# One-hot gather and scatter of a mixture of experts in fp32r, two experts per gather, with the gate applied to the expert's result

## The reference

```
logits = xt @ router_w
top_val, top_idx = top_k(logits, 2)
gates = softmax(top_val)
y_e = (silu(x_e @ w1[e]) * (x_e @ w3[e])) @ w2[e]      # x_e: the tokens that chose expert e
out[token] = sum over its two experts of gate * y_e[token]
```

## Time and profile before

| what | us |
|---|---|
| median of three runs | 2055.57 (2054.56 to 2055.81) |
| profiled execution, first to last instruction (span) | 2052.6 |
| busy: TensorE matmul / VectorE / ScalarE / GpSimd | 1953.8 / 1426.9 / 996.0 / 80.1 |
| expert loop, from the first `up` to the last matmul of the last scatter | 1177.6 to 1995.1 |

### The profile page before, as it was taken

How to read it: one execution, slowest core, us unless ns; L and a number is a source line. 1 busy time by engine, 2 the same in 40 slices (tenths; PEclk the granted TensorE clock), 3 DMA queues, 4 the chain that set the end, 5 groups by cost and what they waited for, 6 DMA issues and landing times. The chain is left out here.

```text
span 2052.6 us, 29833 instructions
## 1 busy us (share of the span) xinstructions
PE 1953.8 (95%) x12519; PEld 1773.6 (86%) x12519; DVE 1426.9 (70%) x1720; ACT 996.0 (49%) x1137; POOL 80.1 (4%) x123
## 2 busy tenths in 40 slices
PE   5988999999998999999999899999999999999998
PEld 4867878878887968999999798989898989898976
DVE  6789996463765346665456488878887888787862
ACT  2511111224366212434355566666666666666654
POOL 3000000000000100100220000000000000000000
PEclk9999999999999999999999999999999999999999
DMA  9845221453432432456753298999898989998970
GB/s 333 267 140 166 85 83 42 156 172 125 143 104 91 158 123 83 145 185 192 211 193 130 95 334 330 342 337 345 333 343 335 341 335 347 333 345 333 342 297 21
DMA packets 225857, 452.29 MB, mean 220 GB/s; under 512 B 6944, under 2 KB 91176, under 8 KB 225720
## 3 DMA queue, kind: packets, MB, share of 16 engines
q1 hardware_dynamic: 222400, 445.44, 61.9%
q0 software_dynamic: 1632, 4.75, 0.8%
q10 hardware_dynamic: 1688, 0.15, 0.1%
HBM read 448.21 MB, written 2.10 MB: 219 GB/s over the span
## 5 line engine op out<-in xcount | busy, mean ns | idle before, releaser
L2002 DVE TENSOR_TENSOR ring_r<-ring,his_r 128x2816 fp32r<-128x2816 f32 (+1 forms) x192 | 586.9, 3085 | 58.4 <-ACT his_r L1543 58.3
L1543 ACT ACTIVATE his_r<-ring 128x2816 fp32r<-128x2816 f32 (+1 forms) x192 | 490.7, 2560 | 193.7 <-DMA ring<-in_moe_w_dram 179.8
L1149 PE MATMUL bank<-his_r,hg_r 128*128 128x352 f32 x2048 | 356.4, 326 | 0.8 <-ACT hg_r L1567 0.8
L1149 PEld LDWEIGHTS bank<-his_r,hg_r 128*128 128x128 f32 x2048 | 334.0, 188 | 1.8 <-issue 0.9
L2475 PE MATMUL bank<-hT,ring 128*128 128x256 f32 x912 | 210.0, 386 | 5.9 <-DVE arena L3053 4.0
L2475 PEld LDWEIGHTS bank<-hT,ring 128*128 128x128 f32 x912 | 171.8, 192 | 33.4 <-issue 10.2
L1149 PE MATMUL bank<-ring_r,hg_r 128*128 128x352 f32 x1024 | 185.9, 323 | 0.0
L1149 PEld LDWEIGHTS bank<-ring_r,hg_r 128*128 128x128 f32 x1024 | 169.0, 188 | 0.0
L3074 DVE SCALAR_TENSOR_TENSOR arena<-ring,cw,arena 128x256 f32<-128x256 f32 x240 | 96.4, 475 | 0.1
L1175 PE MATMUL bank<-his_r,at_hi_r 128*128 128x512 f32 x352 | 93.8, 399 | 0.0
L1175 PE MATMUL bank<-his_r,at_lo_r 128*128 128x512 f32 x352 | 92.5, 396 | 0.0
(11 more groups left out here) (541 smaller groups left out, 2946.1 us busy)
## 6 DMA issues: line engine op xcount, KB each, us to landing
ring<-in_moe_w_dram SPq DMA_DIRECT2D x128, 1408.0 KB, 8.2
ring<-in_moe_w_dram SPq DMA_DIRECT2D x48, 1536.0 KB, 8.7
ring<-in_even_w_in_dram SPq DMA_DIRECT2D x28, 1024.0 KB, 6.5
ring<-in_ffn_w_dram SPq DMA_DIRECT2D x22, 1024.0 KB, 5.3
ring<-in_ada_w_dram SPq DMA_DIRECT2D x20, 1024.0 KB, 10.1
ring<-in_odd_w_in_dram SPq DMA_DIRECT2D x9, 2048.0 KB, 7.8
ring<-in_moe_w_dram SPq DMA_DIRECT2D x16, 1024.0 KB, 6.2
ring<-in_a_w_in_dram SPq DMA_DIRECT2D x6, 2048.0 KB, 8.1
```

Of the source, the lines that this page charges most:

```text
L1149: ins = mm(bank[first + m][:, 0:WC], x[:, KT // 2 * late + k, :], w[:, k, WC * m:WC * m + WC], start=(not late and k == 0 and s == "hg_hi" ...
L1543: A(moe_hi(n), moe_w(n), ACT.Copy).then_inc(sem("moe_hi"), 1)
L2002: V.tensor_tensor(moe_lo(n), moe_w(n), moe_hi(n).bitcast(F32), ALU.subtract).then_inc(sem("moe_lo"), 1)
```

## The change

The gather and the scatter become fp32r products. The tokens are split into `htok_hi_r` (ScalarE) and `htok_lo_r` (GpSimd, four subtractions of 128x512); the one-hot matrix is exact in fp32r. One gather now serves two experts: 256 columns, 32 matmuls, once before the loop and then behind chunk 19 of experts 1, 3 and 5. The scatter multiplies the two parts of the result by a turned one-hot matrix `pick_r`. The gate no longer sits in the matrix: the matrix is turned together with gate columns in a product of 160 columns (`turn_pick`), VectorE sums the gate of each slot (`gate_of_slot`), ScalarE scales by it as it writes the high part of the result, and VectorE makes the low part (`result_lo`). The reciprocals of the router's and the final norm are taken after the turn, over 128x2 instead of 128x256. Before the loop, rank and count products are fewer, `lo(0)`, the gates and the overflow test stand later. The two table loads now count on one semaphore, and both of its readers wait for both loads.

```diff
# SBUF, semaphores of the table loads, GpSimd
+        hg_hi_r = sb_r("hg_hi_r", 0, KT, 2 * SLOTS)
+        hg_lo_r = sb_r("hg_lo_r", 27768, KT, 2 * SLOTS)
+        htok_hi_r = sb_r("htok_hi_r", 4864, TT, D)
+        ys_r = [sb_r("ys_hi_r", 12544, D), sb_r("ys_lo_r", 13568, D)]
...
-            ... a["c_w_s_2"] ... .then_inc(sem("ws_loaded"), 16)
+            ... a["c_w_s_2"] ... .then_inc(sem("spatial_loaded"), 16)
...
-                .then_inc(sem("bs_loaded"), 16)
+                .then_inc(sem("spatial_loaded"), 16)
...
+            for n, (tt, half) in enumerate(TOKEN_ORDER):
+                pool.wait_ge(sem("toks_taken"), TK_H + n + 1)
+                r = slice(512 * half, 512 * half + 512)
+                pool.tensor_tensor(htok_lo_r[:, tt, r], HTOK[:, tt, r], htok_hi_r[:, tt, r].bitcast(F32), ALU.subtract).then_inc(sem("htok_lo"), 1)
# TensorE
-                    pe.wait_ge(sem("ws_loaded"), 16)
+                    pe.wait_ge(sem("spatial_loaded"), 32)
...
+            pe.wait_ge(sem("routed"), 1)
+            mm(bank[1][:, 0:TT * NE], TRI, SEL[:, :, :].rearrange("p u e -> p (u e)"), start=True, stop=False, skip_group_check=True)
+            mm(bank[1][:, NE:TT * NE], ones[:, :], SEL[:, 0, :], start=False, stop=True, skip_group_check=True).then_inc(sem("rank_ready"), 1)
...
+            def gather(n, width):
+                per = 512 // width
                 for ct in range(KT):
+                    if n == 1 and width == 2 * SLOTS and ct % 4 == 0:
+                        pe.wait_ge(sem("htok_lo"), ct // 2 + 2)
...
+                    for x in (htok_hi_r, htok_lo_r):
+                        for tt in range(TT):
+                            ins = mm(o, x[:, tt, ct * P:(ct + 1) * P], s, ...)
...
+            def turn_pick(b, m):
+                for tt in range(TT):
+                    ins = mm(b[:, tt * TURNED:(tt + 1) * TURNED], psel_r[:, tt, m, :], turner_r[:, :], start=True, stop=True)
...
             def scatter(first, done):
                 for ct in range(KT):
-                    ins = mm(bank[first + ct // 2][...], YS[:, ct * P:(ct + 1) * P], GTS, start=True, stop=True)
+                    for y in ys_r:
+                        ins = mm(bank[first + ct // 2][...], y[:, ct * P:(ct + 1) * P], pick_r[...], ...)
...
-                    if j == GATHER_AT and e < NE - 1:
-                        pe.wait_ge(sem("at_lo"), 6 * e + 4)
+                    if j == GATHER_AT and e % 2 == 1 and e < NE - 1:
+                        pe.wait_ge(sem("at_lo"), 6 * e + 6)
+                        pe.wait_ge(sem("psel_ready"), 4 * (e // 2) + 8)
# ScalarE
+            for n, (tt, half) in enumerate(TOKEN_ORDER):
+                act.wait_ge(sem("toks_ready"), TK_H + 4)
+                b, r = bank[(2, 3, 6, 7)[2 * tt + half]], slice(512 * half, 512 * half + 512)
+                A(HTOK[:, tt, r], b[:, :], ACT.Identity, scale=RSC[:, tt:tt + 1])
+                A(htok_hi_r[:, tt, r], b[:, :], ACT.Identity, scale=RSC[:, tt:tt + 1]).then_inc(sem("toks_taken"), 1)
+                if n == 1:
+                    act.wait_ge(sem("routed"), 2)
+                    A(GATE[:, :, :], GATE[:, :, :], ACT.Exp).then_inc(sem("side_exps"), 1)
...
-                    A(YS[...], bank[2 * (e % 2) + half][:, :], ACT.Copy).then_inc(sem("ys_taken"), 1)
+                    A(ys_r[0][...], bank[2 * (e % 2) + half][:, :], ACT.Identity, scale=GSLOT).then_inc(sem("ys_hi"), 1)
# VectorE
-            step(V.reciprocal(nr[:, :], nr[:, :]))
             dve.wait_ge(sem("router_ready"), 1)
-            V.tensor_tensor(RLT[0:NE, :], bank[5][0:NE, 0:T], nr[0:NE, :], ALU.mult).then_inc(sem("norm_scaled"), 1)
-            lo(0)
+            V.tensor_copy(RLT[0:NE, :], bank[5][0:NE, 0:T]).then_inc(sem("norm_scaled"), 1)
             dve.wait_ge(sem("router_ready"), 2)
+            V.reciprocal(RSC, bank[0][:, 2 * NE:2 * NE + TT]).then_inc(sem("norm_scaled"), 1)
...
+            def result_lo(first, n):
+                for half in range(2):
+                    r = slice(512 * half, 512 * half + 512)
+                    dve.wait_ge(sem("ys_hi"), 2 * n + half + 1)
+                    V.scalar_tensor_tensor(ys_r[1][:, r], bank[first + half][:, :], GSLOT, ys_r[0][:, r].bitcast(F32), ALU.mult, ALU.subtract)\
+                        .then_inc(sem("ys_taken"), 1)
...
+            select(0, 0, 0)
+            select(1, 1, 0)
+            dve.wait_ge(sem("rank_ready"), 2)
+            V.tensor_copy(CNT[:, 0, :], bank[0][:, 0:NE]).then_inc(sem("rank_taken"), 1)
+            lo(0)
+            gathered(0)
...
+                    if j == 0 and e >= 1:
+                        result_lo(2 * ((e - 1) % 2), e - 1)
...
-            dve.wait_ge(sem("norm_rooted"), 9)
-            V.reciprocal(nr[:, :], nr[:, :]).then_inc(sem("norm_scaled"), 1)
+            dve.wait_ge(sem("router_ready"), 3)
+            V.reciprocal(RSC, bank[5][:, 0:TT]).then_inc(sem("pair_rooted"), 1)
```

More of the change, by code:

```diff
@@ L91, in build @@
         xT = sb("xT", [P, KT, T])
+        with nc.sbuf_tensor("htok_lo_r", [P, TT, D], F32R) as htok_lo_r:
+            pass
         hT = sb("hT", [P, KT, T])
@@ L94, in build @@
         ones = sb("ones", [P, P])
+        with nc.sbuf_tensor("turner_r", [P, P + 2 * TT * NE], F32R) as turner_r, nc.sbuf_tensor("pick_r", [P, TT, P], F32R) as pick_r:
+            pass
         swap_a = sb("swap_a", [P, P])
@@ L109, in build @@
         stb = segm[:, :]
+        with nc.sbuf_tensor("psel_r", [P, TT, 2, SLOTS], F32R) as psel_r:
+            pass
         hspread = sb("hspread", [P, 2, P])
@@ L1112, in pe_rest @@
-            pe.wait_ge(sem("toks_taken"), TK_H + 4)
-            pe.wait_ge(sem("rank_taken"), 1)
-            def gather(psel, v, done):
-                pe.wait_ge(psel, v)
-                for ct in range(KT):
-                    for tt in range(TT):
-                        ins = mm(bank[6 + ct // 4][:, (ct % 4) * P:(ct % 4 + 1) * P], HTOK[:, tt, ct * P:(ct + 1) * P], PSEL[:, tt, :],
-                                 start=(tt == 0), stop=(tt == 1))
-                    if ct % 4 == 3:
-                        ins.then_inc(done, 1)
+            pe.wait_ge(sem("routed"), 1)
@@ L1125, in scatter @@
+            def turn_pick(b, m):
+                for tt in range(TT):
+                    ins = mm(b[:, tt * TURNED:(tt + 1) * TURNED], psel_r[:, tt, m, :], turner_r[:, :], start=True, stop=True)
+                ins.then_inc(sem("gsel_turned"), 1)
             def scatter(first, done):
                 for ct in range(KT):
-                    ins = mm(bank[first + ct // 2][:, (ct % 2) * T:(ct % 2 + 1) * T], YS[:, ct * P:(ct + 1) * P], GTS, start=True, stop=True)
+                    for y in ys_r:
+                        ins = mm(bank[first + ct // 2][:, (ct % 2) * T:(ct % 2 + 1) * T], y[:, ct * P:(ct + 1) * P],
+                                 pick_r[:, :, :].rearrange("p u t -> p (u t)"), start=(y is ys_r[0]), stop=(y is ys_r[1]))
@@ L1182, in scatter_main @@
                 pe.wait_ge(sem("at_lo"), 6 * e + 6)
-                if e < NE - 1:
-                    pe.wait_ge(sem("hg_lo"), 2 * e + 4)
+                if e % 2 == 1 and e < NE - 1:
+                    pe.wait_ge(sem("hg_lo"), 4 * (e // 2) + 8)
                 scatter(4, sem("scat_ready"))
-            gather(sem("psel_ready"), 2, sem("gather_ready"))
+            pe.wait_ge(sem("psel_ready"), 4)
+            gather(1, 2 * SLOTS)
             for e in range(NE):
@@ L2028, in dve_rest @@
-            dve.wait_ge(sem("gate_exps"), 1)
-            ch.settle()
-            step(V.tensor_tensor(GATE[:, :, :], GATE[:, :, :], SEL[:, :, :], ALU.mult))
-            step(V.tensor_reduce(NEG[:, 0:TT], GATE[:, :, :], AX_X, ALU.add))
-            step(V.reciprocal(NEG[:, 0:TT], NEG[:, 0:TT]))
-            V.tensor_tensor(GATE[:, :, :], GATE[:, :, :], NEG[:, 0:TT].unsqueeze(2).to_broadcast([P, TT, NE]), ALU.mult)\
-                .then_inc(sem("sel_ready"), 1)
-            dve.wait_ge(sem("sel_ready"), 1)
+                .then_inc(sem("routed"), 1)
@@ new lines, in gathered, with gate_of_slot @@
+            def gathered(p):
+                for g in range(4):
+                    dve.wait_ge(sem("hg_hi"), 4 * p + g + 1)
+                    V.tensor_tensor(HG_LO[:, 2 * g:2 * g + 2, :], bank[4 + g][:, :].rearrange("p (k s) -> p k s", k=2),
+                                    HG_HI.bitcast(F32)[:, 2 * g:2 * g + 2, :], ALU.subtract).then_inc(sem("hg_lo"), 1)
+            def gate_of_slot(b, n, e):
+                dve.wait_ge(sem("gts_taken"), n)
+                v = b[:, P:P + TT * (TURNED + 2 * NE)].rearrange("p (u c) -> p u c", u=TT)[:, :, bass.ds(2 * e, 2)]
+                V.tensor_reduce(GSLOT, v, mybir.AxisListType.XY, ALU.add).then_inc(sem("gate_ready"), 1)
@@ new lines, in dve_rest @@
+            select(0, 0, 0)
[4 more added lines that the diff above has]
+            gathered(0)
+            dve.wait_ge(sem("side_exps"), 2)
+            ch.settle()
```

(3 more changed lines are left out.)

197 lines of the change are left out of this document (99 added, 98 removed).

## The result

The kernel after takes 2028.97 us (median of 4 runs, 2024.52 to 2030.28) where the kernel before took 2055.07 beside it (4 runs, 2053.05 to 2055.81): a ratio of 0.9877, 95% interval 0.9865 to 0.9889. The forecast was 2032.0 in a range of 2027 to 2040. The profiled execution has a span of 2027.0 us; against the 2052.6 of before that is −25.6, where the sum said −23.6.

The account below looks back on a forecast made before the run. TensorE was taken to bound the loop, with a chain of waits across engines before and behind it. The terms summed to −23.6 us, from a median of 2055.6 to 2032.0 us, range 2027 to 2040.

Parts of the forecast that it names:

- What bounds the loop: In the expert loop TensorE is busy throughout, 102.4 us per expert, so its work moves the end by its own length.
- (b): In the loop, loads at no more than 347 GB/s become the bound, 99.7 us an expert: +12, 2044; chance 0.06.
- (c): In the loop, loads at 339 GB/s already set the pace and the −24.2 is lost: 2058.6 us; chance 0.02.
- the +0.7 for chunk waits: In the loop, faster slots bring weight loads closer together, so short waits for them add 0.7 us.
- Gathers: In the loop, seven f32 gathers of 3.57 us become three fp32r ones of 3.84: −13.5 us.
- scatters: In the loop, seven scatters go from 3.45 to 1.92 us each: −10.7 us.
- The turned pick: Per expert, two f32 transposes become two fp32r products of 160 columns: 0 change, with +2.7 us kept as possible.
- Rival (a): The narrow product is slow: fp32r at 160 columns costs what f32 does, 2034.7 us; chance 0.35.
- The bias wait: Before the loop, TensorE's transposes wait for both table loads: +2.35 us, plus +0.85 for half a clock drop.
- Ahead of the loop: Routing starts earlier, but the first gather waits for GpSimd's fourth quarter behind `lo(0)`: −0.4 us, between −3 and +2.
- The last scatter: Behind the loop, 0.7 us more wait for the second half, scatter down from 3.73 to 1.92: −1.1 us.
- The final norm: At the end, a 1.76 us reciprocal and 0.18 copy go, a 128x2 reciprocal of 0.17 comes: −1.8 us.

Follow-up runs that it names:

- the narrow gather: Kernel after with each pair's gather cut into 64 products of 128 columns instead of 32 of 256: 2046.96 us, ratio 0.9966.
- f32 scatter: Kernel after with the scatter as one plain f32 product of the result's high part, low part left out: 2038.59 us, ratio 0.9931.
- the run with all idle products: Kernel after with `lo(0)` early, first-load wait only, and unused products during the routing wait and around the last scatter: 2022.35 us, ratio 0.9842.
- the rows stored expert by expert: Kernel after with gathered rows in a separate block per expert instead of 256 columns per pair: 2026.13 us, ratio 0.9867.

## Why the prediction was right, point by point

**What bounds the loop**: right. TensorE is busy throughout the loop, and a piece of it moves the loop's end by its own length, in the narrow gather and the f32 scatter too. Rivals (b) and (c), the loads as the bound, are out: at 358 GB/s TensorE still never waits, and the +0.7 for chunk waits was 0. The Trainium skill ("HBM Reference", the table at its head) gives about 358 GB/s per core; the trace reaches that over a whole expert and goes past it, to 394 in a window of 2.3 us (in the run with all idle products), so it wasn't a limit here.

**Gathers**, forecast −13.5: −12.9, and **scatters**, forecast −10.7: −9.5, both by the start-to-start sums. The forecast took 3.57 and 3.45 us from the chain, which count the slow matmul behind an f32 job; that part now stands in `down` and in `up`. With it the gathers give 12.9 + 0.6 = 13.5 and the scatters 9.5 + 1.3 = 10.8, so the sizes were right. 3.84 and 1.92 us were forecast, 3.83 and 1.90 measured.

**The turned pick**, forecast 0 with +2.7 kept: +0.37 by the table, +0.05 with the 0.32 that stand in `up`. Rival (a) is out. The nearer row was the right choice: 0.09 us at 160 columns (0.11 with what the next matmul loses), 0.111 at 128 in the narrow gather, 0.120 at 256.

**`up` and `down`**, forecast 0: −5.5 and −0.55. Of this 2.2 us are the ends of the f32 jobs, which the forecast had counted with the jobs. The other 3.9 are the step that failed, and it was not one that I had listed: for matmuls of unchanged shape I took unchanged time, though the change moves their weights in SBUF. The place of `hg_lo_r` alone gives 4.0. (`at_lo_r` moved by 256 words too, and its matmuls stayed at 233.3 ns.) Why 27768 is better than the three other places, also in the group that does not read the moved tensor, stays open.

**The bias wait**, forecast +2.35 and +0.85 for the clock: +2.33, and a full drop, +1.7, in the profiled execution. Right in kind; half a drop was somewhat high, since the clock fell in two of six profiled executions with this wait: behind stops of 2.33 and 2.42 us, and not behind 2.05, 1.85, 2.10 and 1.95 (the other kernels with this wait).

**Ahead of the loop**, forecast −0.4: +0.8, inside its range of −3 to +2. The stop behind `lo(0)` was foreseen, though it was the third quarter that stood, for 3.95 us, and not the fourth. Counted from the routing's wait, which starts 3.8 us later than before, the end of the fourth quarter is where the forecast had it (1173.8 forecast, 1173.9 measured), but two errors cancel there. The rank products and the one-hots came 0.7 and 0.6 us later than forecast: I had counted what GpSimd loses to VectorE, but not what VectorE loses to GpSimd, 0.94 us for the comparison that the rank products wait for and 1.12 for the subtraction that stands ahead of the copy of the ranks, 0.17 each without. And a quarter takes 1.26 us, not 1.45. What turned −0.4 into +0.8 stands behind the fourth quarter: 4.4 us to the first `up`, all at the low clock, where I had taken the middle between 2.5 and 4.0. In the runs with the rows stored expert by expert and with the f32 scatter the second half of the gather was at full clock, and the same stretch is 13.96 us, 0.5 less than before.

**The last scatter**, forecast −1.1: this step failed. The wait grew by 1.1 us instead of 0.7, and the scatter fell from 3.7 to 3.3, since it ran at the low clock; with the clock up it took 2.15. But its length does not set when TensorE goes on. From the end of the last `down` to the start of the next product it takes 8.7 to 8.8 us in all eight profiled executions of the kernel after and its variants without products behind the loop, whether the scatter took 2.15 us, 3.4 or, as f32, 3.7, and 7.7 to 7.8 in the five of the kernel before and its variants: +1.0. What ends that wait no trace shows, so the cause stays open. **The final norm**, forecast −1.8: −1.8. The whole stretch behind the last `down` misses by 0.9, and even that flatters the forecast. From execution to execution it differs, with other low stretches of the clock in it each time: 60.7 to 62.5 us in those five executions, 60.4 to 61.7 in seven with the fp32r scatter, 0.5 less in the mean where −2.9 was forecast.

The forecast of 2032.0 is 3 us high: the loop gave 4.6 more than its terms, and the clock, the start and the tail took 2.6 of that back; the rest is the distance of span and median, which is 2.0 in the kernel after for 2.97 in the sum. Without the 3.9 us that the place of a tensor gave, it would have been about 1 us too low.

## What to carry to other kernels

Where one engine is busy from end to end, a forecast by instruction counts and paces from rows is good to a few tenths of a us per term; take paces start to start and keep the handover to the next job apart (0.19 us behind an f32 scatter, 0.08 behind an f32 gather). A GpSimd operation put beside VectorE's chain must be costed in both directions, and moving one long VectorE operation out of its way can be worth more than shortening either (2.0 to 3.3 us here). Before two waits are merged on one semaphore to save one, look at which load lands last and who stands behind the earlier waiter: it cost 1.9 to 2.4 us here, and 1.7 more where the clock fell.

## What was not expected of the hardware

- **The place of a matmul's weights.** The same 3072 `up` matmuls take 501.03 us with `hg_lo_r` at word 1024 or 28160 of the arena, 501.42 at 27776 and 497.03 at 27768, repeatable to 0.01 us. `down` changes by −1.9 to +2.7 ns per matmul with the place of `at_hi_r`.
- **An fp32r product gets little shorter below 256 columns**: 0.09 to 0.11 us at 160 and 128 columns against 0.120 at 256.
- **The first matmul behind a plain f32 job is slow**: 350 ns behind a scatter of 256 columns, 316 behind a gather of 128, for 162 and 237 behind the fp32r ones.
- **A VectorE operation waits for a GpSimd one too**: 0.94 us for 128x16, 0.17 alone; 4.09 us for `lo(0)`, 3.08 alone.
- **A low clock costs little under a wait**: 6.8 us at 1.2 GHz in the first gather cost 0.5 us, the same length behind the last scatter 1.9 (one pair of executions each).
